# Moving the sums of the MLP activations and weights from POOL to DVE, with the up-projections' halves and the down-product loads reordered

## The reference, cut to what matters

```python
merged = gates[:, :, 0] * y_attn + gates[:, :, 1] * y_pool
x = x + jnp.einsum('bsd,de->bse', merged, w_o[l])
h2 = rms_norm(x, norm2_g[l])
u = jnp.square(jax.nn.relu(jnp.einsum('bsd,df->bsf', h2, w_mlp_in[l])))
x = x + jnp.einsum('bsf,fd->bsd', u, w_mlp_out[l])
```

## Time and profile before

| | |
|---|---|
| time, median of 3 runs | 1310.86 us (1310.36 to 1312.37) |
| profiled execution: its time / its span | 1309.64 us / 1307.3 us |
| PE busy | 1269.4 us, 97% |
| DVE busy | 889.5 us, 68% |
| ACT busy | 534.0 us, 41% |
| POOL busy | 358.5 us, 27% |
| mean granted TensorE clock | 0.995 of full |

### The profile page before, as it was taken

One profiled execution on the slowest core, in us unless ns is written; L12 is line 12 of the kernel. 1 busy time (PEld: TensorE's weight loads), 2 busy tenths in 40 slices (PEclk: granted clock), 3 DMA queues, 4 the chain that ended last, 5 costly groups with the idle time before them and its releaser, 6 DMA issues.

```text
span 1307.3 us, 17648 instructions
## 1 busy us (share of the span) xinstructions
PE 1269.4 (97%) x6153; PEld 1063.6 (81%) x6153; DVE 889.5 (68%) x1234; ACT 534.0 (41%) x936; POOL 358.5 (27%) x375
## 2 busy tenths in 40 slices
PE   5999999999899999999999999999998999999998
PEld 5889888887688888887888788888886888888887
DVE  5778777778722222245478877877867998978964
ACT  5556555555311111142245544544454333333330
POOL 3334334333400000000002323332434821606025
PEclk9999999999899999999999999999998999999999
DMA  8010100101111111115222445444539626253223
GB/s 262 17 49 18 44 21 20 36 0 49 33 49 48 48 48 48 64 64 177 81 95 92 155 150 169 150 141 161 168 141 383 245 102 221 96 196 130 95 99 138
DMA packets 106813, 140.65 MB, mean 108 GB/s; under 512 B 4461, under 2 KB 62466, under 8 KB 106754
## 3 DMA queue, kind: packets, MB, share of 16 engines
q1 hardware_dynamic: 106754, 139.88, 31.6%
HBM read 102.12 MB, written 37.75 MB: 107 GB/s over the span
## 4 chain that ended last, share of the span: by engine, by line
PE 86%; DVE 7%; issue 3%; ACT 2%; DMA 1%; POOL 0%; SPq 0%; DVEq 0%; ACTq 0%; POOLq 0%
PE bank L1588 79%; PE bank L1756 2%; PE bank L1685 2%; PE bank L1644 1%; DMA o_raw<-in_w_mlp_out 1%; DVE slot_lo L1049 1%; DVE featT_lo L1330 1%; DMA raw<-in_w_in 1%; ACT slot_hi L712 1%; DVE c L1509 1%; DVE pair_lo L1437 1%; PE bank L1863 1%; PE bank L1739 0%; DVE mixT_lo L1266 0%; DVE wT_lo L1140 0%
## 5 line engine op out<-in xcount | busy, mean ns | idle before, releaser
L1588 PE MATMUL bank<-o_hi,s_hi 128*128 128x512 f32 x448 | 175.5, 392 | 4.8 <-DVE o_lo L1450 4.8
L1588 PE MATMUL bank<-o_hi,s_lo 128*128 128x512 f32 x448 | 175.2, 391 | 0.0
L578 POOL TENSOR_SCALAR small<-small 128x1 f32<-128x1 f32 x80 | 21.2, 265 | 537.4 <-ACT h_row L979 339.0
L1049 DVE TENSOR_TENSOR slot_lo<-raw,slot_hi 128x1024 fp32r<-128x1024 f32 (+1 forms) x45 | 55.2, 1235 | 140.0 <-ACT slot_hi L712 139.5
L1588 PE MATMUL bank<-featT_hi,slot_hi 128*128 128x512 f32 x320 | 127.4, 398 | 0.0
L1588 PE MATMUL bank<-featT_lo,slot_hi 128*128 128x512 f32 x320 | 125.4, 392 | 0.0
L1588 PE MATMUL bank<-featT_hi,slot_lo 128*128 128x512 f32 x320 | 125.1, 391 | 0.0
L1588 PE MATMUL bank<-slot_hi,featT_hi 128*128 128x384 f32 (+1 forms) x320 | 117.9, 368 | 7.3 <-DVE slot_lo L1049 5.3
L1588 PE MATMUL bank<-slot_lo,featT_hi 128*128 128x384 f32 (+1 forms) x320 | 111.7, 349 | 0.0
L1588 PE MATMUL bank<-slot_hi,featT_lo 128*128 128x384 f32 (+1 forms) x320 | 111.5, 349 | 0.0
L1588 PEld LDWEIGHTS bank<-o_hi,s_hi 128*128 128x128 f32 x448 | 84.6, 189 | 23.1 <-DVE o_lo L1450 5.2
(11 more groups left out here) (196 smaller groups left out, 3173.3 us busy)
## 6 DMA issues: line engine op xcount, KB each, us to landing
s_raw<-u_store SPq DMA_DIRECT2D x28, 1024.0 KB, 5.6
pair_raw<-in_w_mlp_in SPq DMA_DIRECT2D x16, 1024.0 KB, 6.1
u_store<-s_tile SPq DMA_DIRECT2D x64, 256.0 KB, 2.1
o_raw<-in_w_mlp_out SPq DMA_DIRECT2D x16, 1024.0 KB, 8.5
raw<-in_w_in SPq DMA_DIRECT2D x28, 512.0 KB, 4.1
u_store<-u_tile SPq DMA_DIRECT2D x48, 256.0 KB, 2.2
x_tile<-in_x SPq DMA_DIRECT2D x8, 512.0 KB, 4.9
res<-in_x SPq DMA_DIRECT2D x8, 512.0 KB, 3.2
```

Source lines behind the costliest of these rows:

```text
L578: pool.tensor_scalar(ms, ss, 1.0 / n_mean, EPS, ALU.mult, ALU.add).then_inc(mean_sem, 1)
L1049: nc.vector.tensor_tensor(slot[1][:, 0:width], raw[r][:, 0:width], slot[0][:, 0:width], ALU.subtract).then_inc(w_ready, 1)
L1588: mm = nc.tensor.matmul(out, a, b, start=start and i == 0, stop=stop and i == len(steps) - 1)
```

## The change

**Sums to DVE.** The `s_tile` sums become `u_sums(p)` on DVE. In iteration `p` of MLP up they are made for the pair before, `u_sums(p - 1)`, between the weight splits of pair `p + 1` and the first `up_add`; those of the last pair come at the start of MLP down. All `o_sums` and the sum of `shared` into `acc` become DVE's too, placed in the loop over the down products.

**Upper half first.** In the loop of up-projections PE and DVE take `i = 1` ahead of `i = 0`, and the last tile's `featT` is split by halves, the upper one first.

**Loads by need.** The first quarter's `o_raw` blocks are loaded in another order into other places, and the second half of the `acc` load goes behind the third `s_raw` load of MLP down.

```diff
-            u11, u21, u22, u12 = u_tile
-            for p in range(PAIRS):
-                pool.wait_ge(u_ready, 4 * p + 2)
-                wait(pool, u_out[1], 16 * p)
-                pool.tensor_tensor(s_tile[0][:], u11[:], u21[:], ALU.subtract).then_inc(s_ready, 1)
...
-            o_sums(0, (2, 3))
-            for t in range(QN):
-                if t == 0:
-                    pool.wait_ge(acc_in[0], 16 * QN)
-                pool.wait_ge(d_added, t + 1)
-                pool.tensor_tensor(acc[:, t, HALVES[0]], acc[:, t, HALVES[0]], shared[:, t, :], ALU.add).then_inc(v_moved, 1)
-            for c in range(1, QUARTERS):
-                o_sums(c, range(4))
...
+            merged_hi(KD - 1, HALVES[1], 2 * KD - 1)
+            split_hi(WO + 4, 0, HEADS + KD + 2, slots[4])
+            merged_hi(KD - 1, HALVES[0], 2 * KD)
...
-                for i in range(2):
-                    merge(d, 0, i, 2 * i)
-                    merge(d, 1, i, 2 * i + 1)
+                for i in (1, 0):
+                    merge(d, 0, i, 2 - 2 * i)
+                    merge(d, 1, i, 3 - 2 * i)
...
+            def u_sums(p):
+
+                u11, u21, u22, u12 = u_tile
+                dve.wait_ge(u_ready, 4 * p + 2)
+                wait(dve, u_out[D7], 16 * p)
+                nc.vector.tensor_tensor(s_tile[0][:], u11[:], u21[:], ALU.subtract).then_inc(s_ready, 1)
...
+                if p > 0:
+                    u_sums(p - 1)
+                if not more:
                     down_lo_o(0)
                     down_lo_s(0)
...
             down_lo_s(1)
-            dve.wait_ge(o_in[0][1], 16)
-            dve.wait_ge(p_done, 7 * PAIRS)
-            nc.vector.tensor_tensor(o_t3[:], o_raw[0][3][:], o_raw[0][1][:], ALU.subtract).then_inc(o_f, 1)
-            dve.wait_ge(o_f, 1)
-            nc.vector.tensor_tensor(o_raw[0][1][:], o_raw[0][1][:], o_raw[0][0][:], ALU.subtract).then_inc(o_f, 1)
+            o_sums(0, (0,))
             down_lo_o(1)
+            u_sums(PAIRS - 1)
+            o_sums(0, (1,))
...
             for n in range(DOWN):
+                c, i = divmod(n, 7)
+                if n == 1:
+                    o_sums(0, (2, 3))
+                if c + 1 < QUARTERS and i == D6:
+                    o_sums(c + 1, (0, 1))
+                if c + 1 < QUARTERS and i == D4:
+                    o_sums(c + 1, (2,))
+                if c + 1 < QUARTERS and i == D5:
+                    o_sums(c + 1, (3,))
...
                 if p == PAIRS - 1:
                     sp.wait_ge(p_done, turn(p, P1))
                     load_s(1)
                     sp.wait_ge(p_done, turn(p, P6))
-                    load_o(0, 2)
+                    load_o(0, 1)
                     sp.wait_ge(p_done, turn(p, P2))
                     load_s(2)
```

More of the change, by code:

```diff
@@ L502, in load_s, with load_acc @@
                 sp.dma_start(s_raw[n % 3][:], u_store[q, 4 * c:4 * c + 4].rearrange("q p c -> p q c")).then_inc(s_in[n % 3], 16)
+            def load_acc(half):
+                for t in range(QN * half, QN * half + QN):
+                    sp.dma_start(acc[:, t, :], res_store[t]).then_inc(acc_in[half], 16)
             def load_o(c, b):
@@ L512, in _ @@
                     load_pair(p + 2)
+                if p == PAIRS - 2:
+                    sp.wait_ge(t_ready, turn(p, P3))
+                    load_o(0, 0)
                 if p == PAIRS - 1:
@@ L910, in _, with merged_hi @@
                     next_tile(d, g)
-            def merged_hi(k):
-                act.wait_ge(merged_ready, 2 * k + 2)
-                nc.scalar.activation(featT[0][:, k, :], mergedT[:, k, :], ACT.Copy).then_inc(m_hi, 1)
+            def merged_hi(k, half, ready):
+                act.wait_ge(merged_ready, ready)
+                nc.scalar.activation(featT[0][:, k, half], mergedT[:, k, half], ACT.Copy).then_inc(m_hi, 1)
             split_hi(WO + 2, 3, HEADS + 2, slots[WO_SLOT[2]], mix_full, 2 * GROUPS)
@@ L1334, in _ @@
             split_lo(WO + 2, 3, slots[WO_SLOT[2]])
[L1335 to L1349 removed]
+            merged_lo(0, ALL, 1)
+            merged_lo(1, ALL, 2)
+            merge(last, 0, 1, 0)
+            merged_lo(2, ALL, 3)
+            merge(last, 1, 1, 1)
+            merged_lo(3, ALL, 4)
+            merged_lo(4, ALL, 5)
+            merge(last, 0, 0, 2)
+            merged_lo(5, ALL, 6)
+            merged_lo(6, ALL, 7)
+            split_lo(WO + 3, 2, slots[WO_SLOT[3]])
+            merged_lo(last, HALVES[1], 8)
+            merge(last, 1, 0, 3)
+            split_lo(WO + 4, 0, slots[4])
+            split_lo(WO + 5, 1, slots[5])
+            split_lo(WO + 6, 3, slots[6])
+            merged_lo(last, HALVES[0], 9)
+            split_lo(WO + 7, 2, slots[7])
             def add_res(s, i):
@@ L1437, in t_split_lo, with o_sums @@
                 nc.vector.tensor_tensor(pair_lo[par][:, i], src, pair_hi[par][:, i], ALU.subtract).then_inc(t_ready, 1)
+            def u_sums(p):
[3 more added lines that the diff above has]
+                nc.vector.tensor_tensor(s_tile[0][:], u11[:], u21[:], ALU.subtract).then_inc(s_ready, 1)
+                dve.wait_ge(u_ready, 4 * p + 3)
+                wait(dve, u_out[D5], 16 * p)
+                nc.vector.tensor_tensor(s_tile[1][:], u21[:], u22[:], ALU.add).then_inc(s_ready, 1)
+                dve.wait_ge(s_ready, 4 * p + 2)
+                wait(dve, u_out[D6], 16 * p)
+                nc.vector.tensor_tensor(s_tile[2][:], u11[:], s_tile[1][:], ALU.subtract).then_inc(s_ready, 1)
+                dve.wait_ge(u_ready, 4 * p + 4)
+                dve.wait_ge(s_ready, 4 * p + 3)
+                wait(dve, u_out[D3], 16 * p)
+                nc.vector.tensor_tensor(s_tile[3][:], u12[:], s_tile[2][:], ALU.add).then_inc(s_ready, 1)
+            def o_sums(c, ks):
+                b11, b12, b21, b22 = o_raw[c % 2]
+                for k in ks:
+                    for b in ((3, 1), (0,), (), (2,))[k]:
+                        dve.wait_ge(o_in[c % 2][b], 16 * (c // 2 + 1))
+                    if c == 0:
+                        dve.wait_ge(p_done, 7 * PAIRS)
+                    else:
+                        dve.wait_ge(d_tile, 28 * (c - 1) + 4 * (D7, D7, D6, D4)[k] + 4)
+                    wait(dve, o_f, 4 * c + k)
+                    out, a, b, op = ((o_t3, b22, b12, ALU.subtract), (b12, b12, b11, ALU.subtract),
+                                     (o_t2, b12, b22, ALU.subtract), (o_t4, b21, o_t2, ALU.add))[k]
+                    nc.vector.tensor_tensor(out[:], a[:], b[:], op).then_inc(o_f, 1)
             def down_lo_o(n):
@@ L1580, in _ @@
                 down_add(n, 3)
+                if n == D7:
+                    for t in range(QN):
+                        c11_t = acc[:, t, HALVES[0]]
+                        dve.wait_ge(d_added, t + 1)
+                        nc.vector.tensor_tensor(c11_t, c11_t, shared[:, t, :], ALU.add).then_inc(v_moved, 1)
         @block.tensor
```

79 lines of the change are left out of this document (21 added, 58 removed).

## The result

The changed kernel takes 1303.33 us (median of 5 runs, 1300.96 to 1304.91) against 1310.36 (5 runs, 1308.83 to 1312.37) for the kernel before on the same chip: ratio 0.9945, 95% interval 0.9929 to 0.9962. Its profiled execution took 1304.91 us with a span of 1303.1, the slowest of its five; it lies 4.7 us under the profiled execution of before, while the medians lie 7.0 apart. Two traces of the changed kernel (the second is among the experiments) differ by 2.0 us in span, and 1.9 of them are one wait of PE. That the same wait spreads the other executions too is likely, but they have no trace.

The account below looks back on a forecast made before the run. PE was taken as the bound, so only its waits could be won. -7.3 (entry to MLP down), -1.1 (first pairs) and +0.6 (output projection) made -7.8, from 1309.64 to 1301.8; 1.22 for the median gave 1303.1, stated as 1303.0; range 1301.3 to 1306.

Parts of the forecast that it names:

- Entry to MLP down, -7.3: At down product 1, earlier `o_raw_1` and `o_lo(1)` remove PE's wait and the low clock: -7.3 us, bounds 0 and 7.3.
- no earlier `o_raw_1`: Rival, entry to MLP down: transfers still queue, only the sum's place gains, PE waits 2 us; 1306 to 1307, chance 0.06.
- Cost taken: 0; if a margin goes, one to three us: Down products 2 to 5: DVE's lo parts come 2 to 3 us before needed; no cost unless a margin fails.
- The margin at product 5: MLP down: DVE has product 5's lo parts at about 1043, PE needs them at 1045.8.
- a wait of PE inside MLP down: Sign that the forecast is wrong: PE waiting anywhere within the MLP down stage.
- half a gain: Rival, down products 2 to 5: a margin fails, PE waits 1 to 3 us; 1304.5 to 1308, chance 0.10.
- the base of the forecast, 1310.86: Starting time for the whole kernel: profiled execution of 1309.64 us, with the median of the runs 1.22 higher.
- MLP down and up in the steady stretches, 0: Steady MLP stages: DVE fits the added sums (66 us of 76 down, 15.2 of 19.04 up), so nothing changes.
- The rival that makes DVE the bound of MLP up: MLP up: if POOL doesn't cause the stretch, a pair takes DVE 20.4 us, over PE's 19.04; 1325, chance 0.05.
- First pairs, -1.1: MLP up's first pairs: DVE's block ahead of `up_add` gets shorter, PE's wait near 727 shrinks; -1.1 us, 0 to -1.7.
- Output projection, +0.6 from -0.2 to +1.1: Start of output projection: last `mergedT` sum comes later, so WO+7's load does; +0.6 us, from -0.2 to +1.1.
- clock fall: Rival, output projection: its short waits also bring the low clock, 2.35 us more; 1305.4, chance 0.06.

Follow-up runs that it names:

- the lower-first one: Changed kernel with the lower half first again in the up-projections and featT split as before the change; 1302.66 us, ratio 0.9931.
- the later one: Comparison in which the changed kernel was run once more, unchanged: 1302.58 us (5 runs, 1301.10 to 1302.86), ratio 0.9936.
- three lower-first experiments: Kernel before with the new loads alone (1308.10 us), with sums moved to DVE alone (1307.06), and changed kernel with lower half first again (1302.66).

## Why the prediction was right, and where it was off

**Entry to MLP down, -7.3: right.** Products 0 to 3 took 10.88 each, with no low clock near, and DVE began `o_lo(1)` 5.2 us after product 0's start (5.3 in the listing). The loads alone won 3.4. The sums alone, which are also the rival "no earlier `o_raw_1`", won 5.3 and gave 5.1 back two products later. It takes the early `o_raw_1`, and beside it either `o_lo(1)` ahead of the in-place sum (shown with POOL's sums running beside it) or DVE without the stretch. The latter is an estimate from after's rows: with the in-place sum first, `o_lo(1)` would have started at about 999.5 and ended at about 1001.8, and PE wanted it at 1002.9. That rival's recorded price doesn't follow from its terms: 3.0 us won of 4.94, and no low clock, make 1305.0, not 1306 to 1307.

**"Cost taken: 0; if a margin goes, one to three us": this is the step that was off.** The margin at product 5 went. It cost 2.50 us in the first profile, 0.6 in the second and 0.2 in the lower-first one; "a wait of PE inside MLP down" is also the recorded sign of being wrong. DVE's operations themselves were counted well. `s_lo(5)` ended at 1048.7; without the 2.58 and 3.67 us in which DVE stood still it would have ended at 1042.5 (an estimate from these rows), where I had 1043, and PE wanted it at 1046.4. So 3.9 us were to spare, and 6.25 went to two late transfers. The working looked at `s_raw(3)` alone and took both as landed in time. The four `acc` loads that the change moves to a later place stand directly ahead of `s_raw(4)`; they put 5.1 us more between the two, and that they are in the way is shown by moving them by one product. It is the rival "half a gain", by its mechanism and within its price of 1 to 3 us, without its low clock; its time, 1304.5 to 1308, holds the profiled execution and not the median.

On the profiled spans the sum is -4.2 where I had -7.8: +2.5 from here, +0.4 from the output projection, +0.65 from the stage start. That the median came out at 1303.33 against 1303.0 is in part luck. The medians lie 7.0 us apart in this comparison and 8.3 in the later one (1310.89 and 1302.58), and the base of the forecast, 1310.86, was 0.5 above the median of before measured beside the changed kernel; the agreement is closer than the working deserves. The lower end of the recorded range, 1301.3, comes out of no sum either: the bounds named give 1301.7.

**MLP down and up in the steady stretches, 0: right.** A pair still takes 19.04 us, DVE's sums fell to 0.69 us and `s_lo` to 2.29. DVE had 70.27 us of 76, not 66: in this window it did 63 operations, not the 54 I had listed, each at its short time. The rival that makes DVE the bound of MLP up is out. With the Trainium skill's rule of contention (GPSIMD Engine Reference, Key points) the traces agree: taking POOL's sums away, or putting them back, changes DVE's `pair_f` sums, with two inputs in SBUF, from 1459 ns to 692 and back, and leaves the readers of PSUM alone. Its factor of two between the engines agrees as well when each works alone: three of POOL's sums that began while DVE stood still took 1.29 us each (before, from 996.35), DVE's take 0.69. The 1682 ns of the earlier trace rows hold POOL's waits for DVE too.

**First pairs, -1.1: right** (-1.05), and due to the `s_tile` sums: with these back on POOL, it is gone.

**Output projection, +0.6 from -0.2 to +1.1: within the bounds, at their upper end** (+1.0). The mechanism is as given. SP issued 7.40 us after the stage's first matmul, where the recorded 593.8 is 7.41 after 586.39; the transfer took 4.2 us and not the middle of the earlier trace rows, and this is the +0.4. No clock fall came. The recorded argument against one, that it took a wait of about 5 us to bring it about, doesn't hold in the trace that it was read from: there the clock also fell at 329.24, behind a wait of 2.24 us, and at 342.89, in one of 2.28. Nor had I weighed the same fall without the change: it came in all three lower-first experiments.

**Start of the output projection, +0.65: not foreseen.** It comes from the first 25 us of the kernel, which the change leaves alone. PE's first matmul behind its wait for ACT's `qkv` starts at 24.84 instead of 24.07, and the lag is 0.82 us at 328.77 and 0.65 here; in the nine traces other than before's it is 0.7 to 1.6 us at the first of these places and 0.4 to 1.3 at the last. PE's longer wait for `mixT_lo`, 3.6 or 3.7 us in these nine against 2.3 before, is not the cause: in before's trace the half clock from 329.24 made PE come later to the same place, and the matmul behind the wait starts at 343.09 before and 343.91 after. Why the first loads' data came later isn't known.

## What to carry to other kernels

When a transfer is moved to a later place, list what now stands behind it in the same queue and when that is wanted; a margin counted from the engine's own operations says nothing until each of its inputs has landed. Two edits on one wait can each look half useful alone (0.9970 and 0.9967 here, 0.9931 together): find the chain of all that ends just ahead of the wait. Sums on a side engine aren't free because it is idle: here the busy engine did them and was busy for less time in total (863.8 us instead of 889.5).

## What the runs showed of the hardware

- **POOL and DVE took turns, one whole operation at a time.** A DVE operation of 128x2048 on two SBUF inputs takes 2.29 us alone, 3.3 to 3.4 beside POOL's 128x512 sums, and up to 5.5 (`s_lo`) and 6.64 (`o_t_lo`) beside its 128x2048 ones. In the MLP stages of before every such DVE operation that was stretched ended 2.15 us after the POOL operation that had been running (19 of 19), and every one of 128x512 0.55 us after it (56 of 56): nearly its own time (2.29 and 0.69), counted anew from POOL's end. In the case below POOL's operation ends at 1011.52 and DVE's at 1013.67:

```profile
1005.05 6.47 POOL L683 TENSOR_TENSOR o_t<-o_raw,o_raw 128x2048 f32<-128x2048 f32 x1 [4.62 <-DVE o_raw L1541]
...
1007.03 6.64 DVE L1450 TENSOR_TENSOR o_t_lo<-o_t,o_hi 128x2048 fp32r<-128x2048 f32 x1
```

The other way round POOL's operation is the one stretched: its 128x512 sum takes 1.29 us alone, 1.68 in the mean and 2.60 to 3.35 beside DVE's operations of 128x2048.

- **The granted clock can fall or not at the same wait.** At the output projection a wait of 2.20 us left the clock at full speed (2.4 GHz) in one trace and was followed by 3.41 us at half (1.2 GHz) in three. In attention a wait of 2.24 us (from 2.23 to 2.25) was followed by such a fall in one trace of ten. Waits of 2.0 and 3.3 us in MLP down were followed by 3.41 us of it too, and the 2.2 us at product 5 by none. The shorter waits at the output projection, 0.8 to 1.5 us and split by matmuls, had none in the six traces with the upper half first.
- **A transfer's landing time is its queue's.** The same load took 5.6 us in the median of its 28, 9.4 with no `acc` loads ahead of it, and 14.7 or 16.6 in two runs of one program behind four others. The four `acc` loads are 2.1 MB and put 5.1 us between two landings (10.5 instead of 5.4), which is about 410 GB/s (an estimate); the windows from 1018 to 1033 of the first profile show 386 to 421.
